# One product for the row shift, and modulation items and weight loads moved around the expert router

## The chip, the cores and the metric

The kernel is one program on one core of a Trainium2 chip. The metric is the device time of one launch in microseconds, the median of three runs. Its engines are TensorE (matrix products and transposes), VectorE, ScalarE, GpSimd and SyncE; SyncE, ScalarE and GpSimd start the transfers between HBM and on-chip memory.

## The reference

One inference step of a backbone with two trunk layers, on 128 context tokens and 512 latent tokens of width 1024:

```
mod = silu(cond) @ mod_w + mod_b          # sh1, sc1, g1, sh2, sc2, g2: 6 x 1024, per group of tokens
h   = rms_norm(x) * (1 + sc1) + sh1       # three mixers: Hyena (two long convolutions), attention, short conv
x   = x + g1 * (merged @ w_o)
h2  = rms_norm(x, norm2_w) * (1 + sc2) + sh2
aff = softmax(h2 @ router_w)              # each of 16 experts takes its best tokens: 16 context, 64 latent
x   = x + g2 * scatter_add(gate * down(silu(a) * u))     # a, u = gathered h2 @ w_gate, w_up
```

The "row shift" is the `+ sh2` of the fourth line, for the rows that are stored to HBM for the experts to gather.

## The kernel before

All weights come from HBM as one stream of items of 128 x 2048 numbers (1 MB), in the order in which TensorE uses them. SyncE asks for them. Four of the places that they land in are `ring`; in the expert stage eight more (`extra`, in the tiles that the trace calls front and back) make it twelve. An item is asked for when the item before it in the same place is used up (`item_used`), and SyncE does so strictly in order.

The kernel runs in stages: a **front** stage, in which the spectra of the long convolutions are made in 20 steps; then for each layer the projections, the attention, the two convolutions (`o` = 0 and 1), the branch and output projections (`w_o`, eight items `c`), the **router** and the 16 **experts** of 6 items each. Between the stages there is no barrier; semaphores set the order, and the code of each engine is written out by hand in the order in which it runs.

The 48 items of `mod_w` (24 per layer) are "modulation items". Each costs TensorE eight 32-column products (`mod_rows`, L777), a copy by ScalarE, and two small products (`mod_columns`, L790 or L792), whose result VectorE or ScalarE adds a bias to. They are needed late, so they are used as filling: `EARLY` of them in the front stage, one or two in each step, and the others (`LATE`, two numbers per layer) in the convolutions and behind the router. The early ones are the 24 of the first layer and those that `LATE` leaves over.

The router stage on TensorE: logits, mean squares, a `spread` of the row scales over all partitions (L758), then ten half tiles of rows. `turn(n)` transposes four 128 x 128 blocks (L1261), `add_shift(n)` adds the shift to them with four full-precision products against diagonal matrices (`diag`, L1267); ScalarE scales the half tile out of PSUM (`evac_t`, L1818), and after each second one stores 128 rows to HBM (`store_rows`, L1824). A `turn` waits until the half tile two before it has been taken out. Meanwhile VectorE finds each expert's best tokens (`best`, `chosen`), which TensorE turns (L1288 to L1294) so that VectorE can write the row numbers `idx`. GpSimd gathers the rows of an expert (L689) when the rows are stored and `idx` is there; `turn_rows` (L1307) turns them, ScalarE and VectorE split them and the weights into a high and a low part, and the expert's products (L1322 to L1352) start.

The router also needs `sh2 @ router_w`: `router_shift` (L1159, sixteen products with 16 columns), which stands between the two halves of the inverse transform of the first convolution (`inverse(0)`, `inverse(1)`, L1174). VectorE takes it into `lbias`.

## Time and profile before

| | |
|---|---|
| median of 3 runs | 2148.35 us (2147.32 to 2151.87) |
| the profiled execution | 2155.39 us, of which 2153.6 us are the span from first to last instruction |
| TensorE busy | 2095.7 us, 97% of the span |
| VectorE, ScalarE, GpSimd busy | 1681.4, 1134.5, 164.2 us |
| moved by the DMA engines | 435.80 MB, 202 GB/s on average |
| granted TensorE clock, mean | 0.989 of full |

A busy TensorE is a TensorE with work in its pipeline; it says nothing of how densely the products follow each other. What a stage is worth is read from its own timeline.

### The profile page before, as it was taken

Reading aid. Unit: us, or ns where it says so; the run is one execution under the profiler, and the core shown is the slowest. Engines: PE = TensorE matmul, PEld = TensorE weight load, DVE = VectorE, ACT = ScalarE, POOL = GpSimd, SP = SyncE. Lnnn points to the kernel's source line nnn. Section 1 sums busy time; section 2 is a strip of 40 time slices with the busy share of each in tenths; the row PEclk is TensorE's granted clock in tenths of the full one; section 3 lists DMA queues with packets and bytes.
Section 4 is the critical chain, followed back from the end, with each engine's and each line's share of the span. In section 5 each row is a group of like instructions: output and inputs, shape, how many; then the busy total and the mean of one; then the engine's idle time right before and its main releaser. Section 6 shows DMA issues by size and latency. Waiting matters only on the chain.

```text
span 2153.6 us, 35885 instructions
## 1 busy us (share of the span) xinstructions
PE 2095.7 (97%) x13286; PEld 1707.6 (79%) x13286; DVE 1681.4 (78%) x2516; ACT 1134.5 (53%) x1798; POOL 164.2 (8%) x192
## 2 busy tenths in 40 slices
PE   8999999999999999999999999999999999999999
PEld 3449999998768997666668999999766999666666
DVE  7767878876768645999997787887777764799997
ACT  5434444324712255888884444433651225788884
POOL 1110000001001100111100000000100100111110
PEclk9999999999999999999999999999999999999999
DMA  9982433213133517999992243222413434999995
GB/s 334 329 305 87 147 136 119 83 75 117 76 118 136 171 62 294 392 382 385 382 354 98 96 147 133 98 82 76 152 42 135 159 130 159 353 378 385 385 386 216
DMA packets 76975, 435.80 MB, mean 202 GB/s; under 512 B 9228, under 2 KB 9900, under 8 KB 36381
## 3 DMA queue, kind: packets, MB, share of 16 engines
q1 hardware_dynamic: 54336, 352.87, 42.7%
q0 software_dynamic: 19024, 72.32, 10.7%
q10 hardware_dynamic: 3470, 8.64, 1.1%
q8 instruction: 96, 1.57, 0.3%
q14 instruction: 49, 0.40, 0.1%
HBM read 384.95 MB, written 48.84 MB: 201 GB/s over the span
## 4 chain that ended last, share of the span: by engine, by line
PE 80%; DVE 8%; ACT 4%; issue 4%; DVEq 2%; DMA 2%; ACTq 0%; POOL 0%; another core or an unknown queue 0%; POOLq 0%
PE ps L738 21%; PE ps L977 17%; PE ps L1322 9%; PE ps L1348 5%; PE ps L1326 4%; PE ps L919 3%; PE ps L1352 2%; PE ps L843 2%; PE ps L1049 2%; DMA kspec<-back 2%; PE ps L777 2%; PE ps L1174 2%; PE ps L1177 1%; PE ps L933 1%; PE ps L1102 1%
## 5 line engine op out<-in xcount | busy, mean ns | idle before, releaser
L738 PE MATMUL ps<-front_r 128*128 128x320 f32 x2432 | 417.0, 310 | 1.6 <-DVE back_r L2474 0.8
L738 PEld LDWEIGHTS ps<-front_r 128*128 128x128 f32 x2432 | 370.1, 188 | 3.0 <-DVE back_r L2474 1.4
L1420 ACT ACTIVATE front_r<-ring 128x1024 fp32r<-128x1024 f32 (+1 forms) x216 | 182.5, 845 | 261.2 <-PE ps L738 172.1
L977 PE MATMUL ps<-back_r,front_r 128*128 128x320 f32 x1728 | 265.1, 309 | 0.0
L977 PEld LDWEIGHTS ps<-back_r,front_r 128*128 128x128 f32 x1728 | 256.4, 188 | 0.0
L1420 ACT ACTIVATE back<-ps 128x512 f32<-128x512 f32 (+5 forms) x206 | 98.5, 496 | 249.6 <-PE ps L738 114.1
L977 PE MATMUL ps<-front_r 128*128 128x320 f32 x1296 | 204.7, 311 | 5.3 <-DVE back L2153 5.1
L977 PEld LDWEIGHTS ps<-front_r 128*128 128x128 f32 x1296 | 191.9, 188 | 10.4 <-DVE back L2153 9.5
L1420 ACT ACTIVATE front_r<-back 128x512 fp32r<-128x512 f32 (+2 forms) x216 | 150.1, 709 | 87.8 <-PE ps L977 35.0
L2588 DVE TENSOR_TENSOR back_r<-front,back_r 128x1024 fp32r<-128x1024 f32 x128 | 153.5, 1220 | 12.4 <-ACT back_r L1420 10.6
L1322 PE MATMUL ps<-back_r 128*80 128x512 f32 x384 | 152.3, 397 | 3.7 <-ACT back_r L1420 3.7
L1322 PE MATMUL ps<-back_r,front_r 128*80 128x512 f32 x384 | 152.3, 397 | 0.0
L738 PE MATMUL ps<-back_r,front_r 128*128 128x320 f32 x640 | 145.8, 309 | 0.0
L2137 DVE TENSOR_TENSOR front_r<-back,front_r 128x512 fp32r<-128x512 f32 x144 | 98.8, 686 | 55.3 <-ACT front_r L1420 55.1
L1420 ACT ACTIVATE back_r<-front 128x1024 fp32r<-128x1024 f32 x128 | 132.9, 1055 | 5.8 <-PE ps L1326 1.0
L1921 DVE TENSOR_TENSOR front_r<-ring,front_r 128x1024 fp32r<-128x1024 f32 x76 | 92.8, 1223 | 42.9 <-ACT front_r L1420 41.8
L1326 PE MATMUL ps<-back_r 128*80 128x512 f32 x384 | 120.5, 395 | 0.0
L2588 DVE TENSOR_TENSOR back_r<-ring,back_r 128x1024 fp32r<-128x1024 f32 x96 | 114.3, 1218 | 2.5 <-ACT back_r L1420 1.2
L738 PEld LDWEIGHTS ps<-back_r,front_r 128*128 128x128 f32 x640 | 107.1, 188 | 0.0
L1348 PE MATMUL ps<-back_r,front_r 128*80 128x512 f32 x384 | 105.7, 397 | 0.0
L1420 ACT ACTIVATE back_r<-ring 128x1024 fp32r<-128x1024 f32 x96 | 99.6, 1055 | 7.1 <-PE ps L1352 4.1
L2153 DVE TENSOR_TENSOR back<-ps,back 128x320 f32<-128x320 f32 x180 | 88.2, 490 | 14.7 <-PE ps L977 2.1
(317 smaller groups left out, 3734.8 us busy)
## 6 DMA issues: line engine op xcount, KB each, us to landing
ring<-in_stream SPq DMA_DIRECT2D x186, 1024.0 KB, 7.9
front<-in_stream SPq DMA_DIRECT2D x80, 1024.0 KB, 16.0
back<-in_stream SPq DMA_DIRECT2D x48, 1024.0 KB, 14.9
gates<-back SPq DMA_DIRECT2D x24, 640.0 KB, 3.1
back<-gates POOLq DMA_DIRECT2D x48, 320.0 KB, 3.3
kspec<-back POOLq DMA_DIRECT2D x20, 512.0 KB, 8.4
front<-kspec POOLq DMA_DIRECT2D x8, 1024.0 KB, 7.7
rows<-front ACTq DMA_DIRECT2D x10, 520.0 KB, 5.4
```

Source lines behind the costliest of these rows:

```text
L738: mm = pe.matmul(tokh(b)[:, c0:c1], w(wp)[:, k, :], src(hp, k)[:, c0:c1], start=first, stop=last)
L777: mm = pe.matmul(ps[32 * j:32 * j + 32, row_bank(i), 0:256], cs[:, k, :], w[:, k, :], start=k < 4, stop=k >= 4)
L919: mm = pe.matmul(qkv_tile(i, t), h_part(hp, 4 * hf + k)[:, P * t:P * t + P], w2(hf, 4, wp)[:, k, :], start=first and hf == 0 and t % 2 == ...
L977: mm = pe.matmul(ps[:, bank, 0:TH], w[:, wp, k, :], x(k), start=k == 0 and wp == 0 and x is hi and j not in (2, 6), stop=k == 3 and wp == ...
L1322: pe.matmul(ps[0:SLOTS, hf, :], x[:, k0 + k, :], hi[:, k, :], start=k0 + k == 0 and x is xe_hi, stop=False)
L1326: mm = pe.matmul(ps[0:SLOTS, hf, :], xe_hi[:, k0 + k, :], lo[:, k, :], start=False, stop=k0 + k == KC - 1)
L1348: pe.matmul(ps[0:SLOTS, 6 + c, :], hidT[i][:, ee % 2, 2 * half + k, :], hi[:, k, :], start=half + k + i == 0, stop=False)
L1420: return act.activation(o, i, ACT.Copy)
L1921: dve.tensor_tensor(half_dst(u, 1), src, half_dst(u, 0).bitcast(F32), ALU.subtract).then_inc(w_lo, 1)
L2137: dve.tensor_tensor(WG[:, n % 4, 1, :], operand(l, n), WG[:, n % 4, 0, :].bitcast(F32), ALU.subtract).then_inc(w_lo, 1)
L2153: dve.tensor_tensor(out[:, dst, :], ps[:, bank, 0:TH], out[:, one, :], ALU.add).then_inc(gate_dve, 1)
L2588: dve.tensor_tensor(w[:, 1, :], part_item(l, ee, v)[1], w[:, 0, :].bitcast(F32), ALU.subtract).then_inc(e_wlo, 1)
```

## The change

It has five parts.

1. The shift of the rows becomes one product. Every number of `sh2` lies in a 16-partition pattern `shift_rows` (made by one product at the end of `router_shift`, with ScalarE copying its operand and VectorE its low part); VectorE spreads it into `spread_rows` at the fourth output item with two products of 96 x 1024. `add_shift` is then one product of the reduced-precision type fp32r with 512 columns, its 96 rows holding high and low parts. The sixteen `diag` activations per layer on ScalarE go. The low part of the spread row scales is a new VectorE operation ahead of the search.
2. `router_shift` moves behind `inverse(1)`, and VectorE's `lbias` copies behind the four products that follow it.
3. SyncE asks for 3 instead of 6 expert items before it waits for the first gather.
4. `LATE` gives the router stage of the first layer 6 instead of 4 modulation items; `EARLY` falls from 29 to 27. The lists of one and two items per step in the front's steps 10 to 19 change from 1 2 2 1 2 2 1 2 2 2 to 1 2 1 2 1 2 1 2 1 2.
5. Three modulation items stand between the last row and the turned places, the others behind them, and then 4 (first layer) or 10 (second) products whose result nobody reads (`keep_busy`).

```diff
-MODS, LATE = DEPTH * N_MOD, ((5, 4), (6, 4))
+MODS, LATE = DEPTH * N_MOD, ((5, 6), (6, 4))
...
+        with nc.sbuf_tensor("shift_rows", [P, QK], F32R) as shift_place:
+            pass
+        shift_rows = shift_place[:, P:2 * P]
...
+        shift_cols = qkw[:, 2 * P:3 * P]
...
-        z, spr, diag = region(56, [KC, T]), region(86, [T]), region(76, [2, KC, P])
+        z, spr, spread_rows = region(56, [KC, T]), region_r(86, [T]), region_r(76, [2, KC, P])
...
                 for x in range(LAP):
-                    if x == 6:
+                    if x == 3:
 
                         sp.wait_ge(gathered[0], l * 64 + 16)
...
-                                mm = pe.matmul(ps[:, 7, 320 + NE * g:320 + NE * g + NE],
+                                pe.matmul(ps[:, 7, 320 + NE * g:320 + NE * g + NE],
                                                mod[:, l, 24 + k, g:g + 1].to_broadcast([P, P]), rw[:, k, :],
                                                start=k == 0, stop=k == KC - 1)
-                        mm.then_inc(r_lg, 1)
+                        pe.wait_ge(sh_hi, 2 * l + 1)
+                        pe.matmul(ps[:, 7, 0:P], shift_cols, ident[:], start=True, stop=True).then_inc(r_lg, 1)
...
                     else:
                         prompt_inverse(0)
+                        pe.wait_ge(rt_lo, 3 * l + 1)
                     forward_second()
...
                     inverse(0, range(4))
                     if o == 0:
                         prompt_forward()
+                    inverse(1, range(4))
+                    if o == 0:
                         router_shift()
-                    inverse(1, range(4))
...
                 def add_shift(n):
                     t, hf = n // 2, n % 2
-                    for i in range(4):
-                        mm = pe.matmul(ps[:, 4 + n % 2, P * i:P * i + P], spr[:, P * t:P * t + P],
-                                       diag[:, int(t > 0), 4 * hf + i, :], start=False, stop=i == 3)
-                    mm.then_inc(t_ready, 1)
+                    pe.matmul(ps[:, 4 + n % 2, :], spr[0:96, P * t:P * t + P],
+                              spread_rows[0:96, int(t > 0), 4 * hf:4 * hf + 4, :].rearrange("p i n -> p (i n)"),
+                              start=False, stop=True).then_inc(t_ready, 1)
...
-                pe.wait_ge(z_ready, l * Z_IN + Z_IN)
+                pe.wait_ge(rt_lo, 3 * l + 3)
                 add_shift(0)
                 add_shift(1)
...
-                pe.wait_ge(r_places, l * 2 + 1)
-                apart(pe)
-                pe.transpose(ps[0:SLOTS, 0, 0:LISTS], places[:], ident[0:LISTS, 0:LISTS])
...
+                def turn_places():
+                    pe.wait_ge(r_places, l * 2 + 1)
...
                 mods = late_mods(l, 1)
-                for i in mods:
+                for x, i in enumerate(mods):
+                    if x == 3:
+                        turn_places()
                     mod_rows(i)
-                    if i > mods[0]:
+                    if x:
                         mod_columns(i - 1)
                 mod_columns(mods[-1])
+                keep_busy(2, 10 if l else 4)
...
                     if o:
+                        act.wait_ge(r_lg, 2 * l + 1)
+                        copy(shift_rows, ps[:, 7, 0:P]).then_inc(sh_hi, 1)
                         act.wait_ge(y_sum, l * 4 + 1)
...
                     late_add(conv_mods(l, o)[-1])
+                    if o == 0:
+                        act.wait_ge(modcol_read, conv_mods(l, o)[-1] + 1)
+                        copy(shift_cols.rearrange("p (j m) -> p j m", j=8), mod[:, l, 24:32, :].rearrange("p k g -> p (k g)")
+                             .unsqueeze(1).to_broadcast([P, 8, 16])).then_inc(sh_hi, 1)
...
-                        act.activation(diag[:, g, k, :], ident[:], ACT.Identity, scale=mod[:, l, 24 + k, g:g + 1])
...
-                    if o == 0:
-                        dve.wait_ge(r_lg, 2 * l + 1)
-                        for g, t0, t1 in ((0, 0, 1), (1, 1, NT)):
...
                     for m in range(4):
                         dve.wait_ge(y_inv, l * 10 + 5 * o + m + 1)
...
                         ins.then_inc(y_out, 1)
+                    if o == 0:
+                        dve.wait_ge(r_lg, 2 * l + 1)
+                        dve.wait_ge(sh_hi, 2 * l + 2)
...
+                        dve.tensor_tensor(shift_rows[64:96, :], ps[64:96, 7, 0:P], shift_rows[64:96, :].bitcast(F32),
+                                          ALU.subtract).then_inc(rt_lo, 1)
...
                 for c in range(KC):
+                    if c == 3:
+                        whole = [96, KC, P]
+                        for g in range(2):
+                            ins = dve.tensor_tensor(spread_rows[0:96, g], shift_rows[0:96, :].bitcast(F32).unsqueeze(1).to_broadcast(whole),
+                                                    sel16[0:96, g:16:2].unsqueeze(2).to_broadcast(whole), ALU.mult)
+                        ins.then_inc(rt_lo, 1)
...
+                dve.wait_ge(z_ready, l * Z_IN + Z_IN)
+                dve.tensor_tensor(spr[32:64, :], spread_at(l, 1)[32:64, :], spr[32:64, :].bitcast(F32),
+                                  ALU.subtract).then_inc(rt_lo, 1)
                 dve.wait_ge(r_affT, l + 1)
```

TensorE around `router_shift` in the first layer (`ps` is PSUM), before:

```order
L1174 MATMUL ps<-front 128x512 x8
L1138 MATMUL ps<-back,csi 128x512 x2
L1159 MATMUL ps<-rw,mod 128x16 x16
L1174 MATMUL ps<-front 128x512 x8
L1102 MATMUL ps<-back,front 128x256 x16
```

and after:

```order
L1180 MATMUL ps<-front 128x512 x8
L1143 MATMUL ps<-back,csi 128x512 x2
L1180 MATMUL ps<-front 128x512 x8
L1164 MATMUL ps<-rw,mod 128x16 x16
L1168 MATMUL ps<-ident,qkw 128x128
L1107 MATMUL ps<-back,front 128x256 x16
```

The sixteen products now follow both inverse halves, with one more behind them.

TensorE from the last half tile of rows to the first gathered rows, first layer, before:

```order
L1261 MATMUL ps<-ident,back 128x128 x4
L1267 MATMUL ps<-back 128x128 x4
L1288 MATMUL ps<-ident,places 80x80
L1289 MATMUL ps<-ident,best 64x80
L1294 MATMUL ps<-back 64x32
L777 MATMUL ps<-ring,cs 32x256 x16
L792 MATMUL ps<-sel,back 128x2 x2
L777 MATMUL ps<-ring,cs 32x256 x8
L792 MATMUL ps<-sel,back 128x2 x2
L777 MATMUL ps<-ring,cs 32x256 x8
L792 MATMUL ps<-sel,back 128x2 x4
L1307 MATMUL ps<-ident,back 128x80 x8
```

and after, from the third modulation item on; three of them now come ahead of the places and three behind, then the four `keep_busy` products, and each group of four shift products has become one (`L1274 MATMUL ps<-back_r 128x512`):

```order
L782 MATMUL ps<-ring,cs 32x256 x8
L797 MATMUL ps<-sel,back 128x2 x2
L1296 MATMUL ps<-ident,places 80x80
L1297 MATMUL ps<-ident,best 64x80
L1302 MATMUL ps<-back 64x32
L782 MATMUL ps<-ring,cs 32x256 x8
L797 MATMUL ps<-sel,back 128x2 x2
L782 MATMUL ps<-ring,cs 32x256 x8
L797 MATMUL ps<-sel,back 128x2 x2
L782 MATMUL ps<-ring,cs 32x256 x8
L797 MATMUL ps<-sel,back 128x2 x4
L771 MATMUL ps<-csi,ident 128x256 x4
```

SyncE's requests from the last items of the trunk on, with what they wait for, before:

```order
L548 DMA ring<-in_stream 128x2048 [waits item_used] x27
L548 DMA front<-in_stream 128x2048 [waits merge_ready]
L548 DMA front<-in_stream 128x2048 x2
L548 DMA back<-in_stream 128x2048 x3
L548 DMA ring<-in_stream 128x2048 [waits r_sub,rows_stored,item_used,t_evac,gathered0]
L548 DMA ring<-in_stream 128x2048 [waits item_used] x3
L548 DMA front<-in_stream 128x2048 x2
```

and after:

```order
L553 DMA ring<-in_stream 128x2048 [waits item_used] x29
L553 DMA front<-in_stream 128x2048 [waits merge_ready]
L553 DMA front<-in_stream 128x2048 x2
L553 DMA back<-in_stream 128x2048 [waits rows_stored,r_sub,t_evac,gathered0]
L553 DMA back<-in_stream 128x2048 x2
L553 DMA ring<-in_stream 128x2048 [waits item_used] x4
L553 DMA front<-in_stream 128x2048 x2
```

The first row has two more modulation items, and the wait for the gather has moved three items ahead.

## Rows read from the trace of the kernel before

**Rows 1.** TensorE timeline in the front stage: start, duration, line, form, idle before

```profile
114.33 1.07 PE L777 MATMUL ps<-ring,cs 128*32 128x256 f32 x16 [0.48 <-ACT back L1420]
...
129.87 0.41 PE L790 MATMUL ps<-ident,back 128*128 128x128 f32 x2 [1.23 <-DVE mod L1975]
...
134.64 0.44 PE L790 MATMUL ps<-ident,back 128*128 128x128 f32 x2
```

**Rows 2.** TensorE timeline, second half of the first convolution and start of the next

```profile
623.71 3.87 PE L1159 MATMUL ps<-rw,mod 128*128 128x16 f32 x32
...
627.42 8.57 PE L1174 MATMUL ps<-front 128*128 128x512 f32 x16
...
635.83 7.07 PE L1102 MATMUL ps<-back,front 128*128 128x256 f32 x32
```

**Rows 3.** stretches: busy us of PE, PEld, DVE, ACT, POOL; PEclk, DMA share, GB/s

```profile
627.00:630.00 3.00, 3.00 (x7) 1.57 (x7) 1.36 (x4) 0.00 (x0) 0.71 (x1) 0.50 0.82 329
...
821.00:824.00 3.00, 3.00 (x18) 3.00 (x18) 1.79 (x9) 1.83 (x4) 0.00 (x0) 0.59 1.00 423
...
842.00:845.00 3.00, 2.90 (x40) 1.81 (x39) 0.00 (x0) 1.21 (x5) 1.46 (x2) 1.00 0.10 15
...
849.00:851.00 2.00, 1.05 (x3) 0.72 (x4) 1.95 (x3) 2.00 (x3) 0.00 (x0) 0.50 1.01 296
```

**Rows 4.** VectorE timeline, end of the second spectrum half

```profile
623.10 1.22 DVE L2414 TENSOR_TENSOR front<-back 128x1024 f32<-128x1024 f32 x1
```

**Rows 5.** VectorE timeline at the fourth output item

```profile
787.92 1.01 DVE L1956 SCALAR_TENSOR_TENSOR X<-ps,mod,X 128x128 f32<-128x128 f32 x2 [3.81 <-PE ps L738]
```

**Rows 6.** TensorE timeline of the router stage, first layer

```profile
828.46 0.60 PE L1261 MATMUL ps<-ident,back 128*128 128x128 f32 x4
...
828.89 1.06 PE L1267 MATMUL ps<-back 128*128 128x128 f32 x8
...
837.77 0.23 PE L1288 MATMUL ps<-ident,places 80*80 80x80 f32 x1
...
842.05 1.07 PE L777 MATMUL ps<-ring,cs 128*32 128x256 f32 x16
...
843.71 1.07 PE L777 MATMUL ps<-ring,cs 128*32 128x256 f32 x16
...
847.31 0.77 PE L1307 MATMUL ps<-ident,back 80*128 80x80 f32 x8 [0.16 <-issue]
...
849.95 0.71 PE L1322 MATMUL ps<-back_r 128*80 128x512 f32 x1 [1.86 <-ACT back_r L1420]
...
852.59 0.63 PE L1322 MATMUL ps<-back_r 128*80 128x512 f32 x1
```

**Rows 7.** ScalarE timeline of the same stage: first pair of rows, last store

```profile
826.33 1.52 ACT L1818 ACTIVATE front<-ps,rstd 128x512 f32<-128x512 f32 x2 [2.12 <-PE ps L1267]
...
838.74 0.33 ACTq L1824 DMA_DIRECT2D rows<-front  x1
```

**Rows 8.** VectorE timeline of the same stage

```profile
825.38 0.42 DVE L2541 COPY back<-ps 80x256 f32<-80x256 f32 x1 [1.18 <-PE ps L1276]
...
837.27 0.17 DVE L2552 CAST places<-chosen 16x16 f32<-16x16 uint32 x1
...
839.41 0.17 DVE L2568 SCALAR_TENSOR_TENSOR idx<-ps,back 64x16 uint32<-64x16 f32 x1
```

**Rows 9.** GpSimd timeline: the first gather of rows

```profile
843.24 0.99 POOL L689 DMA_INDIRECT back<-rows,idx  x1 [94.26 <-DMA rows<-front]
```

**Rows 10.** SyncE timeline: the last two weight items of the first layer

```profile
1097.22 1.70 SPq L583 DMA_DIRECT2D front<-in_stream  x2
```

**Rows 11.** DMA issues of 1098 to 1100: size, time from issue to landing

```profile
front<-in_stream SPq DMA_DIRECT2D x1, 1024.0 KB, 19.8
```

**Rows 12.** TensorE timeline: the first product of the last item

```profile
1129.83 1.13 PE L1348 MATMUL ps<-back_r,front_r 128*80 128x512 f32 x4
```

**Rows 13.** TensorE timeline: the first rows turned for an expert, second layer

```profile
1848.00 0.75 PE L1307 MATMUL ps<-ident,back 80*128 80x80 f32 x8
```

26 lines of the change are left out of this document (15 added, 11 removed).

## The prediction

> **What bounds the kernel now.** I read the profile's page first: TensorE is busy for 97% of the span, so a gain has to come out of its timeline or out of something that it waits for. Then the timelines of TensorE stage by stage, beside them those of the engines that release it, and last the transfers.
>
> In the front stage TensorE is the bound, with stalls on top. A modulation item costs it 1.28 us there (114.33 to 115.33 for the eight products, and the two small ones take it to the next product 0.27 us later), and in the later steps it waits 0.48 us for ScalarE and 1.23 us for VectorE [rows 1]. In the convolution it runs without a gap: `router_shift` takes 3.7 us, `inverse(1)` 8.4 us, and the next transform follows at once [rows 2]. The granted clock was 0.50 from 627 to 630, that is 1.2 instead of 2.4 GHz, right behind the sixteen narrow products [rows 3]. The operand of `inverse(1)` was ready only at 624.32 [rows 4]. At the output items VectorE idles 3.8 us in 7 [rows 5].
>
> In the router stage I look for what comes last ahead of the first expert product. A half tile costs TensorE 0.43 us for `turn` and 0.90 us for `add_shift` [rows 6], 13.3 us for ten; ScalarE takes 0.76 us per half tile and about 0.4 us for a store, so it waits for TensorE; the last store is asked for at 838.74 [rows 7]. VectorE starts the search at 825.38, has the places at 837.4 and `idx` at 839.6 [rows 8]; GpSimd starts to gather only at 843.24, released by the last store [rows 9]. So the rows come last, by 3.6 us. The gathered rows are turned at 847.31, the first expert product starts at 849.95, and the clock is 0.50 there [rows 3, 6]. In the expert stage TensorE never waits for weights. But the last item, asked for at about 1098.7 [rows 10], lands 19.8 us later [rows 11], at 1118.5, for a product at 1129.83 [rows 12]; its ScalarE and VectorE passes take some 1.8 us ahead of it (the low part is needed later), so the stream has only 9.5 us to spare. In the second layer the same stage starts at 1848.00 [rows 13], and I take its slack as the first's.
>
> **The change part by part.**
>
> *Two items fewer in the front.* 2 x 1.28 = 2.6 us of TensorE. The two stalls, 1.7 us together, lie in steps behind the removed items, and 2 MB less are in flight by then; I take 1.4 of them. Sum -4.0; ends -2.6 (TensorE alone) and -7 (the same relief once more elsewhere).
>
> *`router_shift` behind `inverse(1)`.* TensorE's work is the same plus one full-precision product of 128 columns, 0.23 us by the four in 0.90 us [rows 6]. But `inverse(1)` would start at 623.87 and its operand is there at about 624.45: 0.6 us of idle time that `router_shift` covered. The slow spell cost about 1.7 us of the work behind it (3.4 us at half speed); it can land on the next transform in the same way, or not come. I take +0.3 per layer, +0.6 in all; ends -0.5 and +1.2 per layer. The new waits: ScalarE stands at `r_lg` with only its copy of the spectrum behind it, which waits for TensorE's transform, 3.5 us later, anyway. VectorE's copies and its low part (about 0.5 us) fall in the same pause. Cost nothing.
>
> *The spreading on VectorE*, twice 96 x 1024: 2.4 us, since an operation on 128 x 1024 takes 1.22 us [rows 4], and it fits under 3.8 us of idle time [rows 5]. The `diag` activations that go were hidden too. Both nothing; without the cover +2.4 per layer.
>
> *One product per half tile.* A product of 512 columns in fp32r is paced at 0.23 us [rows 12]: TensorE needs 0.43 + 0.23 = 0.66 us, and ScalarE becomes the bound with 2.0 us per pair including the store. It starts 0.6 us earlier and takes 10 us: last store at 835.4 instead of 838.74. GpSimd saw the stored rows 4.5 us after the last request, so now at 839.9 instead of 843.24. The new VectorE operation (640 columns, 0.8 us at the pace of [rows 4]) fits into the 1.2 us that VectorE waits ahead of 825.38.
>
> *Three modulation items ahead of the places.* They pace at 1.66 us each, 842.05 to 843.71. TensorE is free at 834.2, ScalarE's first copy waits for its last store, so the third ends at 839.5; the places were ready at 837.4. The places are turned 1.7 us later than at 837.77, `idx` comes at 841.3, and the gather starts at about 841.6. Now `idx` comes last, 1.6 us earlier than the rows did. The places' own late turn is what is next in line.
>
> *What follows them.* First layer: three more items, 840.5 to 846.6, then four products of 256 columns at 0.44 us (16 take 7.1 in L1102's rows, 0.44 each [rows 2]): TensorE reaches `turn_rows` at 848.3, the gathered rows are there by 845.7 if the gather takes 4.1 us as before (843.24 to 847.31), by 847.5 beside five loads. +1.0 against 847.31. Second layer: one item and ten such products, 847.6: -0.5 against 1848.00.
>
> *The clock.* Before, TensorE idles much between 845 and 850, and the first two weight parts then take 2.64 us each (849.95 to 852.59 is the first) [rows 6]. Six products at 0.23 would take 1.4, and VectorE's pass over a part 1.2: 2.5 us lost per layer. The added products fill the idle time up to the turned rows, but 1.9 us without any product remain behind them. I take -1.7 per layer, nearer to the whole since one slow spell may stay; ends 0 and -2.5. The Trainium skill (TensorE: Matmul & The Clock Gate, Loop structure matters more than you think) says that a copy out of PSUM by VectorE between groups of products does not make the array go cold, while a wait for a DMA does. By that the whole 2.5 would come back, -1.6 us more in all; no row before shows it or excludes it, and it is part of the rival "more".
>
> *The held items.* An item is 1.05 MB at 423 GB/s, 2.5 us [rows 3]. Second layer: three items not there beforehand are 7.5 us, the gather comes 1.2 us earlier, so the stream ends 6.3 us later, TensorE's need is 2.2 us earlier: 8.5 of 9.5 us. No wait. First layer: five (two of modulation), 12.5 us, of which the DMA engines' pause before (15 GB/s from 842 to 845 [rows 3]) gives back some 5: 7.5 to 9, against 9.5 - 0.7. I take +0.3 and +0.5 for the partial sums, which are loaded behind the last item. The Trainium skill (DMA: Bandwidth & Descriptors, Where 436 GB/s comes from) puts the HBM side of one core at about 358 GB/s. By that an item would take 2.9 us and the five of the first layer 2.1 us more, which comes out as waiting; it speaks for the rival "eaten up". The trace has 423 GB/s, and the measurement decides.
>
> Sum: -4.0 + 0.6 + (1.0 - 1.7 + 0.8) + (-0.5 - 1.7) = -5.5 us. The profiled execution would be 2155.4 - 5.5 = 2149.9; it lies 7 us over the median of the runs shown, so for the median I take the difference: 2148.35 - 5.5 = **2142.9**.
>
> **The rivals.** 0.2% (4.3 us) is about what a measurement of this kernel tells from no change.
>
> *Eaten up.* The stream is the bound of the first layer: the gather shares the engines with five loads, lands at 849.5, and the end waits 3 us; the clock falls as before in both layers. For it: 9.5 us of slack against 7.5 to 9. Against it: TensorE is not free before 848.3 anyway. -4.0 + 0.6 + (2.2 + 3.0) + (-0.5) = +1.3 with no clock back, -4.0 + 0.6 + (1.0 - 1.0 + 3.0) + (-0.5 - 1.0) = -1.9 with some: about 2147 (2145 to 2150).
>
> *The rows stage goes cold (slower).* TensorE ran through the rows without a pause; now it waits a third of a microsecond for ScalarE in each half tile. The clock fell behind narrow products and pauses three times in these rows (0.50 at 627, 0.59 at 821, 0.50 at 849) [rows 3]; whether short regular pauses do it too, no row shows. If they do, `turn` and product take 1.3 us, the rows end 3.5 us later than I say, and each of the three items ahead of the places takes 2.0 us instead of 1.0 in its products, 3 us more. Then the places are turned at 846 instead of 837.8, and the gather starts 5 us later than at 843.24, in both layers: -4.0 + 0.6 + 2 x 5 = +6.6, 2155. Against it: the clock was full from 827 on, through transposes and modulation items with pauses of their own. It decides only if both layers' stages are slow throughout; one alone ends at +1.6.
>
> *More.* Both spells of the convolutions vanish (-0.5 each instead of +0.3), the clock comes back whole, the front gives 6: -6 - 1.0 + (1.0 - 2.5 + 0.8) + (-0.5 - 2.5) = -10.7: 2137.7.
>
> **How the numbers follow.** Forecast (2139 to 2146) 0.50; eaten up 0.28; cold rows 0.12; more 0.10. The range from 2137 to 2150 leaves out the cold rows and a little of the last. Faster by over 0.2% (under 2144.05): 0.45 of the forecast and 0.10, 0.55. Within: 0.05 and 0.28, 0.33. Slower: 0.12.
>
> **What the profile of the changed kernel would show.** Right: the spread product 0.23 us per half tile, half tiles 1.0 us apart with ScalarE as releaser, the last store near 835.4 on this scale, the places turned about 839.5, the first gather released by VectorE and not by a store, an expert stage that starts at a granted clock of 1.00 or falls to 0.50 more briefly; the front 4 us shorter; latencies of the last weight items near 27 us and still no wait for a landing. Wrong: a clock of 0.50 between 825 and 845; expert products that wait for weight passes held up by a transfer; a gather still released by a store.

## The result

The changed kernel is slower: 2161.97 us (median of 4, 2160.24 to 2163.45) against 2147.84 us (median of 4 on the same chip). The ratio is 1.0058 with a 95% interval of 1.0046 to 1.0071. By the ratio that is 12.5 us, and the two medians lie 14.1 us apart, where -5.5 was forecast. Its profiled execution took 2160.24 us, with a span of 2158.4. The execution of before whose rows stand above was one of its longest (2155.39 us), so the two traces differ by less, 4.8 us, and only that much (8.6 us against the second profile) can be followed stage by stage. A second profile of the kernel before (2151.59 us, span 2149.8) stands beside it in this table; the times are starts of TensorE's instructions, in us.

| | before, rows above | before, second profile | after |
|---|---|---|---|
| first layer: places turned | 837.8 | 837.0 | 835.2 |
| gathered rows turned | 847.3 | 847.5 | 847.4 |
| first expert product | 849.95 | 850.16 | 850.55 |
| last expert product | 1133.8 | 1133.8 | 1137.8 |
| second layer: places turned | 1837.9 | 1835.8 | 1842.9 |
| gathered rows turned | 1848.0 | 1844.5 | 1852.6 |
| last expert product | 2134.2 | 2130.4 | 2139.0 |

So the lead of 3.0 us (2.3 against the second profile) with which the changed kernel comes to the first router stage is gone between the places and the first expert product. From the turned places to the turned rows it takes 12.2 us, where before took 9.5 and 10.5. The expert stage then takes 287.3 us instead of 283.8 and 283.6. In the second layer the way from the places to the rows is 9.7 us, where before took 10.1 and 8.6.

**What the changed kernel's profile shows.** SyncE's timeline (start, duration of the group, line, tile, number of transfers) in the first layer:

```profile
803.29 30.24 SPq L553 DMA_DIRECT2D ring<-in_stream  x3
833.58 1.57 SPq L553 DMA_DIRECT2D front<-in_stream  x3
846.70 1.28 SPq L553 DMA_DIRECT2D back<-in_stream  x3
```

The three `ring` transfers were asked for over 30 us: the first at 803.29, the other two, modulation items five and six, not before 831.4 and 833.2. The expert items behind them on the queue follow at 833.58. What the transfers did meanwhile is in the stretches (length, TensorE busy, granted clock, DMA share, GB/s), first of the changed kernel:

```profile
808.00:831.00 23.00, 21.34 (x165) 0.93 0.21 84
831.00:850.00 19.00, 14.40 (x132) 0.81 1.00 353
```

The same stretches in the second profile of before:

```profile
808.00:831.00 23.00, 22.48 (x180) 0.93 0.70 281
831.00:850.00 19.00, 13.78 (x148) 0.96 0.71 242
```

From 808 to 831 the changed kernel moved 84 GB/s (the stores of the rows, nearly all of it) where before moved 281. From 831 on its engines are full, just when the gather comes. GpSimd's timeline at the first gather:

```profile
837.90 1.02 POOL L694 DMA_INDIRECT back<-rows,idx  x1 [91.91 <-DVE idx L2596]
```

The DMA issues (transfers, KB each, us to landing) of 833.4 to 835:

```profile
front<-in_stream SPq DMA_DIRECT2D x3, 1024.0 KB, 15.1
```

And those of 837.5 to 838.5:

```profile
back<-rows,idx POOLq DMA_INDIRECT x1, 8.8
```

The gather is asked for at 837.90, released by VectorE's `idx` and no longer by a store [rows 9]. It takes 8.8 us to land, and an expert item takes 15.1 us (the middle one of three). TensorE's timeline shows what the stage makes of that:

```profile
830.25 1.07 PE L782 MATMUL ps<-ring,cs 128*32 128x256 f32 x16
...
835.21 0.24 PE L1296 MATMUL ps<-ident,places 80*80 80x80 f32 x1
...
838.47 1.07 PE L782 MATMUL ps<-ring,cs 128*32 128x256 f32 x16 [0.69 <-DMA ring<-in_stream]
...
840.81 1.07 PE L782 MATMUL ps<-ring,cs 128*32 128x256 f32 x16 [0.73 <-DMA ring<-in_stream]
...
843.86 3.76 PE L771 MATMUL ps<-csi,ident 128*128 128x256 f32 x8
847.41 1.27 PE L1318 MATMUL ps<-ident,back 80*128 80x80 f32 x8
850.55 0.71 PE L1333 MATMUL ps<-back_r 128*80 128x512 f32 x1 [1.86 <-ACT back_r L1431]
...
852.34 1.05 PE L1337 MATMUL ps<-back_r 128*80 128x512 f32 x2
```

The two late modulation items wait for their own transfers (0.69 and 0.73 us). The filling products, four of 256 columns in eight records, take 3.76 us, twice the 1.76 of the prediction, because they ran at half clock. The gather had landed at 846.68, 0.7 us before the rows were turned at 847.41: it was TensorE's own chain that came last. The granted clock in these stretches, and in those of the second layer:

```profile
840.00:843.00 3.00, 1.69 (x21) 0.97 1.02 406
843.00:850.00 7.00, 5.67 (x20) 0.50 1.03 308
1843.00:1846.00 3.00, 2.05 (x25) 1.00 0.00 0
1846.00:1850.00 4.00, 3.90 (x12) 0.57 0.57 137
```

The first layer's spell at 0.50 began at 842.8 and lasted 13.7 us, where before had 6.8 from 848.8. TensorE had not stood for more than 0.8 us at a time in the ten microseconds ahead of its fall. In the second layer's timeline the ten filling products (20 records) end behind the landing of the first gathered rows, which was at 1849.70:

```profile
1846.75 6.03 PE L771 MATMUL ps<-csi,ident 128*128 128x256 f32 x20
1852.62 0.72 PE L1318 MATMUL ps<-ident,back 80*128 80x80 f32 x8
```

In the expert stage ScalarE now waits for weights. Its waits from 850 to 1135 (released by, us in total, times, longest):

```profile
ACT back_r L1431 <- DMA ring<-in_stream: 4.1, 3, 1.6
...
ACT back_r L1431 <- DMA back<-in_stream: 1.4, 3, 0.8
```

No such wait is in either profile of before. TensorE's timeline where the longest of them reaches it:

```profile
1045.80 1.14 PE L1359 MATMUL ps<-front_r 128*80 128x512 f32 x4 [1.19 <-DVE front_r L2633]
```

The stages that came nearest to what was foreseen are the front and the convolution. TensorE's timeline in the front:

```profile
109.53 0.41 PE L795 MATMUL ps<-ident,back 128*128 128x128 f32 x2 [0.52 <-DVE mod L1991]
...
127.24 0.41 PE L795 MATMUL ps<-ident,back 128*128 128x128 f32 x2 [1.70 <-DVE mod L1991]
...
131.01 0.50 PE L825 MATMUL ps<-b,rows 40*128 40x512 f32 x2
```

And in the first layer's convolution:

```profile
620.39 7.13 PE L1180 MATMUL ps<-front 128*128 128x512 f32 x16 [0.50 <-DVE front L2430]
627.36 3.64 PE L1164 MATMUL ps<-rw,mod 128*128 128x16 f32 x32
...
631.16 8.76 PE L1107 MATMUL ps<-back,front 128*128 128x256 f32 x32
```

There are still two such stalls as in [rows 1], 0.52 and 1.70 us, and TensorE's waits up to 140 us are no shorter in sum (12.6 us; 12.4 and 11.9 before). The product that stands at 131.01 stood at 135.01 in the rows above, but at 132.60 in the second profile of before. `inverse(1)` waits 0.50 us and the narrow products still bring the clock down, now over the next transform, which takes 8.76 us instead of 7.07 [rows 2].

### The profile page after: what moved, and what is told of

It is laid out like the page before. It is cut to its first block, busy times and chain, and to the rows that moved or that the text cites. A ratio compares the mean times of both kernels' runs of the same rounds, so it can differ in the third digit from the quotient of the medians.

```text
span 2158.4 us, 35657 instructions
## 1 busy us (share of the span) xinstructions
PE 2095.1 (97%) x13182; PEld 1702.1 (79%) x13182; DVE 1686.5 (78%) x2520; ACT 1126.0 (52%) x1774; POOL 165.8 (8%) x192
## 4 chain that ended last, share of the span: by engine, by line
PE 71%; DMA 9%; DVE 8%; ACT 5%; issue 4%; DVEq 3%; ACTq 0%; POOL 0%; SPq 0%; POOLq 0%
PE ps L743 21%; PE ps L982 17%; PE ps L1333 6%; PE ps L1359 4%; DMA ring<-in_stream 3%; PE ps L1337 3%; PE ps L924 3%; DMA back<-in_stream 2%; DMA kspec<-back 2%; PE ps L1363 2%; PE ps L1054 2%; PE ps L1183 1%; DMA front<-in_stream 1%; PE ps L848 1%; PE ps L1107 1%
## 5 line engine op out<-in xcount | busy, mean ns | idle before, releaser
L2616 DVE TENSOR_TENSOR back_r<-front,back_r 128x1024 fp32r<-128x1024 f32 x128 | 153.5, 1221 | 12.5 <-ACT back_r L1431 10.7
```

The source lines that it names most:

```text
L2616: dve.tensor_tensor(w[:, 1, :], part_item(l, ee, v)[1], w[:, 0, :].bitcast(F32), ALU.subtract).then_inc(e_wlo, 1)
```

## The experiments

All ratios are to the kernel before, timed in turn with it on the same chip. Runs that are compared with each other were not always on one chip, so they are compared by their ratios. 0.1% is 2.15 us. The "held items" are the expert items that SyncE asks for ahead of its wait for the first gather. In the later groups "bare" means without the filling products and with `router_shift` between the transforms again.

**e1_before**: the kernel before once more.

> The kernel before, unchanged, for a second profile on this chip. Its first profiled execution took 2155.39 us and the median of the others was 2148. If the difference of 7 us is a stage of its own (a slower stream, one more spell at half clock), it shows when the two traces are laid side by side: the stage in which they part is where executions of this kernel differ. Expected: 2148, parted from the first profile in the expert stages or in the number of spells at half clock.

Its profiled execution took 2151.59 us. The two traces of one kernel lie 2.4 us apart at the end of the front stage, level again in the first expert stage, 1.6 us apart at the second convolution, 2.0 at the second layer's rows and 3.6 at its gathered rows. The spells at half clock are not the same either: one at 612.9 is new, one at 1613.4 is gone. So an execution's place in 2147.5 to 2155 is made of many small waits and spells, no single stage. One profile against one profile can't tell less than some 5 us here, and the verdicts below go by the ratios.

### The queue: six modulation items and four slots

```diff
 # e4_ahead: the changed kernel, three held items ahead of modulation items five and six
+                    if l == 0 and g >= first - 2:
+                        continue
                     load(g)
...
                     if x == 3:
+                        if l == 0:
+                            load(first - 2)
+                            load(first - 1)
                         sp.wait_ge(gathered[0], l * 64 + 16)
 # e5_four_more: the kernel before with LATE = ((5, 6), (6, 4))
 # e13_four_more_behind: the same with the edit of e4_ahead, at x == 6
 # e2_four: the changed kernel with LATE = ((5, 4), (6, 4))
 # e3_six_held: the changed kernel with x == 6
```

> The changed kernel with one thing moved on SyncE's queue: in the first layer the three held expert items are asked for ahead of modulation items five and six instead of behind them. Bytes, items and TensorE's order are the same. 'Held back': the three land by 832 as before, 7.5 us of stream are won in the pause from 808 to 831, the gather has two items ahead of it instead of five and lands in 4 to 6 us instead of 8.8 to 12.9; TensorE starts the expert stage 1 to 3 us earlier and does not wait for the stream (-3.4): -4.5 to -6.5, about 2156.5. 'Volume': no difference, 2162. 'Clock': no difference, the products that fill are there as before, within 1 us of 2162.

Measured: 1.0019 (1.0010 to 1.0029), 2154.7 us. The order of five transfers on one queue is worth 0.39%, 8 us, with no byte and no product changed. SyncE's timeline:

```profile
801.21 0.33 SPq L553 DMA_DIRECT2D ring<-in_stream  x1
810.98 1.28 SPq L553 DMA_DIRECT2D front<-in_stream  x3
829.38 2.16 SPq L553 DMA_DIRECT2D ring<-in_stream  x2
840.11 1.28 SPq L553 DMA_DIRECT2D back<-in_stream  x3
```

The three expert items are asked for at 811 and not at 833.6. The gather, asked for at 835.91, landed at 840.09, in 4.2 us instead of 8.8, and in the whole expert stage ScalarE waits for no landing. TensorE itself did not turn the rows before 846.09, since modulation item six (1.63 us late) and the fill lay ahead of them. Its timeline:

```profile
839.09 1.07 PE L786 MATMUL ps<-ring,cs 128*32 128x256 f32 x16 [1.63 <-DMA ring<-in_stream]
...
842.54 3.76 PE L775 MATMUL ps<-csi,ident 128*128 128x256 f32 x8
846.09 1.14 PE L1322 MATMUL ps<-ident,back 80*128 80x80 f32 x8
849.09 0.46 PE L1337 MATMUL ps<-back_r 128*80 128x512 f32 x1 [1.86 <-ACT back_r L1435]
```

The places were turned at 833.21, so the way to the rows is 12.9 us, no shorter than the changed kernel's 12.2, though the gather took half the time. What the order gave back in this trace is the expert stage: 283.0 us instead of 287.3.

> The kernel before with nothing changed but the place of two modulation items: six in the first layer's router stage instead of four, 27 in the front. 'Held back': -4.0 in the front, but the six expert items wait behind items five and six, whose slots come free only behind the places, at about 840; they land from 845 on, the gather lies behind eight transfers, TensorE gets the first weights and the rows some 10 us late and the stream bounds the stage: +5 or more in all, 2153 or more. 'Volume': 5 us of stream out of 9.5 us of slack, no wait: -4, 2144.

Measured: 1.0045 (1.0032 to 1.0059). Two items moved on the kernel before cost 10 us, with the front's gain already taken off. SyncE stood from 802.2 to 835.8, the gather took 11.4 us, the first expert product came at 853.0, and the expert stage took 289.4 us, with 8.1 us of ScalarE's waits for landings.

> e5_four_more (1.0045) with all six held expert items asked for ahead of modulation items five and six. Two items more in the first layer's router stage, on the kernel before, with nothing else in their way but the ring's slots. 'Held back': the expert items land by 832 as before, the two late modulation items are asked for at 836 to 838 and the gather shares the engines with them: turned 2 to 4 us later than before, front -4: ratio 0.999 to 1.000. If it stays at 1.0045, the order on SyncE's queue is not what e5_four_more lost, but the two items' own work and bytes.

Measured: 1.0016 (1.0006 to 1.0026). The same two items with the queue in order: 6 us better, ScalarE waits for no weights, but not the gain that I expected. In its trace, that of the longest of its eleven executions, the gather still takes 7.7 us beside the two late items and the rows are turned 15.4 us behind the places (9.5 before): TensorE waits 2.49 us for item six and turns the rows 2.1 us after they have landed. Both readings hold in part: 0.29% is the order, the rest the two items themselves, their transfers and TensorE's wait for them.

> The changed kernel with four modulation items in the first layer's router stage again (29 in the front), all else as changed. Theory 'held back': SyncE issues the stream in order, the ring has four slots, and items five and six wait for a slot that TensorE frees only behind the rows, so the expert items behind them are late (their first landing was at 849.3 where before it was at 820.9). Four items fit the ring: the first expert items are asked for at about 816 again, the gather lands in 4 us, no product waits for the stream. Against the changed kernel +4.0 in the front, -3.4 in the expert stage, -3 ahead of the first expert product: about -2.5, 2159.5. Rival 'volume' (two items more, three not held: the bytes are what is late): the same two items leave the expert stage, -3.4, and nothing ahead of it: +0.6. Rival 'clock' (the products that fill the wait run at half speed and cost more than the wait): +4.0 alone, 2166.

Measured: 1.0026 (1.0015 to 1.0038), 7 us under the changed kernel. I expected 2.5 and the sign is right. The first layer's gather landed in 3.97 us. The expert stage still took 286.4 us, and ScalarE waited 4.6 us for landings. The first layers of e6_no_fill and e7_conv, also with three held, took 286.1 and 286.3 us; with four held and the same four modulation items it was 282.9 to 284.7 (b2, e11, e12, e15). e4_ahead took 283.0 with three, but its first expert product came 9.0 us after the gather had landed, where e2_four's came after 2.8. So three held items are too few for the stream once TensorE comes early.

> The changed kernel with six expert items ahead of SyncE's wait again instead of three. 'Held back': the three more cannot be asked for before modulation item six has its slot, at 833 to 835, so they lie ahead of the gather (asked for at 837.9) with 7.5 us of transfers: the gather lands near 854 instead of 846.7, the first expert product comes 3 to 6 us later, and the stream, which then never pauses for the gather, gives back the 3.4 us of waits: 0 to +3 against the changed kernel, 2162 to 2165. 'Volume' (three items fewer in advance are what the stream lacks): -3.4, about 2158.5.

Measured: 1.0045 (1.0029 to 1.0062), against 1.0058. That is nearer to what 'volume' said (1.0042) than to 'held back' (1.0058 or more), and the interval reaches both. Items four to six were not asked for before 836, as foreseen, but the gather did not wait for them: it took 8.5 us, hardly less than beside the five, and the way from places to rows stayed at 12.3 us. My theory had the gather 7 us later, and that was wrong. The stream still bounded the expert stage (286.4 us, 3.7 us of ScalarE's waits).

### The filling products, the convolution

```diff
 # e6_no_fill: e2_four without
-                keep_busy(2, 10 if l else 4)
 # e7_conv: e2_four with router_shift() ahead of inverse(1) again
```

> Four modulation items in the first layer, and the products that fill the wait for the gathered rows left out (they compute nothing that is used). Compared with e2_four (1.0026 of before). 'The fill is in the way': in the second layer of e2_four the gathered rows landed at 1846.98 and TensorE turned them only at 1852.90, behind ten such products in 7.6 us at half clock; in the first layer the rows landed at 844.36 and were turned at 844.40. So -4 to -6 from the second layer, nothing from the first: ratio to before about 1.0002. Rival 'the fill keeps the clock': without it the expert stages start at half clock for 2.5 us longer in both layers: +3 and -5 give -1 to -2, ratio about 1.0018.

Measured: 1.0017 (1.0008 to 1.0026), 2 us under e2_four, with intervals that overlap. That is the rival's number (1.0018). In the trace the second layer's way from places to rows fell from 12.6 to 6.8 us; the same trace has 13.7 us at 0.50 from 1838.6, and its expert stage is 1.0 us longer. So one trace shows the fill in the way and some of it paid back by the clock, but by the times its going is worth 0.09%, which the error covers.

> Four modulation items in the first layer, and the products of the router's shift between the two inverse transforms again instead of behind the second; compared with e2_four (1.0026). There TensorE waited 0.50 us ahead of the second inverse transform in the first layer and the narrow products brought the half-clock spell all the same, now over the next transform: 1.0 us lost in the first layer and some 1 to 1.5 in the second. Back in the old order: -2, ratio about 1.0017. Rival (the price lies in the added product and the new waits of ScalarE and VectorE, whatever the place): 0, ratio 1.0026.

Measured: 1.0019 (1.0011 to 1.0028), again 1.5 us under e2_four and inside its interval. From the second half's first transform to its last the first layer took 21.7 us in four of five runs with the new order (20.1 in the fifth) and 21.0 in most with the old one, but 22.4 to 22.7 in three; the second layer 21.0 to 23.8 and, but for one, 20.7 to 22.6. By the means the move costs 0.15 us in the first layer and 1.2 in the second, too little to be shown by a time.

### The one product alone: what a pause costs

```diff
 # e9_product: bare, four modulation items, six held, and turn_places() ahead of all of them
+                turn_places()
                 for x, i in enumerate(mods):
-                    if x == 3:
-                        turn_places()
 # e10_third_six: the same with turn_places() behind the third item
 # e11_first_four: e9_product with x == 4
 # e14_filled_pause: e9_product with
+                keep_busy(2, 9)
                 turn_places()
```

> The one product per half tile alone on the kernel before: four modulation items in the first layer, all of them behind the places, six expert items held, the router's shift between the inverse transforms, nothing that fills. TensorE has the rows done some 5 us earlier. Theory 'the stores queue behind the held items': with six items asked for ahead of them the last store took 10.46 us to land in b1_six_ahead (asked for at 830.52, landed 840.99), against 2.65 us for most stores with three held; so the gather starts hardly earlier than before, 1 us at most per layer: -1 to -2, ratio 0.9992. Rival 'the rows came last' (as the prediction had it): gather 1.6 to 3 us earlier per layer, the modulation items behind the places end at the same time as the rows land: -4 to -5, ratio 0.998.

Measured: 1.0040 (1.0028 to 1.0052). Both theories fell: less work for TensorE made the kernel 8.6 us slower. TensorE's timeline in the second layer:

```profile
1829.90 0.47 PE L1274 MATMUL ps<-back_r 96*128 96x512 f32 x1
1834.57 0.33 PE L1296 MATMUL ps<-ident,places 80*80 80x80 f32 x1 [4.19 <-DVE places L2578]
...
1835.81 1.93 PE L782 MATMUL ps<-ring,cs 128*32 128x256 f32 x16
1838.34 1.94 PE L782 MATMUL ps<-ring,cs 128*32 128x256 f32 x16 [0.59 <-ACT back L1429]
...
1848.29 1.31 PE L1316 MATMUL ps<-ident,back 80*128 80x80 f32 x8
```

The rows are done at 1830.3, the places come from VectorE at 1834.6. TensorE stood for 4.19 us, and from 1833.7 the granted clock was 0.50 for 20.5 us: a modulation item's products take 1.94 us where they took 1.07, four items take until 1848, and the rows that landed near 1842.6 wait for them.

> e9_product with one thing changed: three modulation items ahead of the places instead of none (six expert items held, four modulation items in the first layer, nothing that fills, the router's shift between the transforms). Theory 'TensorE idles behind the rows': in e9_product it stood 4.3 us before the places, the clock was 0.50 from 833.6 to 840.4 and from 847.3 to 854.1 in the first layer and for 20.5 us from 1833.7 in the second, and the modulation items and the first weights ran at half speed; with the items in that pause the spells are shorter and most of the 8 us come back: ratio 1.000 to 1.0015. Rival 'the price is in the product and its helpers' (copies, spreading, new waits): 1.0040 as e9_product.

Measured: 0.9998 (0.9988 to 1.0007). Three modulation items in the pause, nothing else changed, are worth 0.42%.

> b2_four_held (0.9987) with one thing changed: the places ahead of all four modulation items, so e9_product with four held expert items instead of six. 'TensorE idles behind the rows': the pause of 4.3 us is there again, the clock falls: ratio 1.002 to 1.004. Rival 'the stores behind the held items' (what e9_product lost lies in the six held): 0.998 to 0.999, as b2_four_held or better, since the places are turned 1 us earlier.

Measured: 1.0039 (1.0024 to 1.0053). With b2_four_held (0.9987, below) this makes a square: places first 1.0040 and 1.0039, places third 0.9998 and 0.9987, at six and four held. The pause is the price; the stores behind six held items instead of four cost some 0.1%, with intervals that overlap.

> e9_product (1.0040) with nine products that nobody uses in TensorE's pause between the last row and the places: 9 x 0.44 = 4.0 us at the full clock, in a pause of 4.3 us. No work that counts is moved: the four modulation items stay behind the places. If the clock is what the pause costs, most of it comes back: ratio 1.000 to 1.001, as e10_third_six (0.9998), and the spells at half clock behind the pause get shorter. If e10_third_six gained because three modulation items lie out of the way of what follows the places (5 us of work earlier), this one stays at 1.0035 to 1.0045.

Measured: 1.0006 (0.9998 to 1.0015). Four microseconds of products that nobody uses make e9_product 7 us faster. No other work moved, so it is the clock. By the traces nearly all of it is in the second layer, where the way from the places to the first expert product falls from 16.9 to 12.4 us; in the first layer it is 12.8 and 13.0, since the rows there were ready only 1.0 us before e9_product turned them. The same timeline:

```profile
1828.47 4.05 PE L771 MATMUL ps<-csi,ident 128*128 128x256 f32 x18
1832.68 0.24 PE L1296 MATMUL ps<-ident,places 80*80 80x80 f32 x1 [0.16 <-DVE places L2579]
...
1833.65 1.07 PE L782 MATMUL ps<-ring,cs 128*32 128x256 f32 x16
1835.31 1.07 PE L782 MATMUL ps<-ring,cs 128*32 128x256 f32 x16 [0.59 <-ACT back L1430]
...
1841.91 1.33 PE L1317 MATMUL ps<-ident,back 80*128 80x80 f32 x8 [0.40 <-DMA back<-rows,idx]
```

The stretch from 1833 to 1854 (columns as above) in e9_product:

```profile
1833.00:1854.00 21.00, 15.93 (x98) 0.52 0.75 272
```

and in e14_filled_pause:

```profile
1833.00:1854.00 21.00, 17.01 (x123) 0.84 0.78 283
```

The granted clock is 0.52 against 0.84. The items take 1.07 us again and TensorE is at the rows when they land.

### Toward a version that keeps the gains

```diff
 # b1_six_ahead: bare, six modulation items, six held items ahead of the last two of them
 # b3_ahead_bare, b4_ahead_four: the same with three and with four held
 # b2_four_held: bare, four modulation items, four held (x == 4)
 # e12_second_four: b2_four_held with turn_places() behind the second item
 # e15_short_fill: b2_four_held with keep_busy(2, 4) behind the last item
```

> What the theory would keep: the one product per half tile and six modulation items in the first layer, but all six held expert items asked for ahead of modulation items five and six, no products that fill, and the router's shift between the inverse transforms. Against e4_ahead (1.0019): -3 from the second layer's fill, -2 to -3.5 from the first's (rows landed at 840.1, turned at 846.1), -2 from the convolutions, and three items more in hand for the stream: ratio 0.9975 to 0.9985, about 2146. If the stream is what bounds it even so, ratio 1.000.

Measured: 1.0014 (1.0005 to 1.0023), no gain: with six transfers ahead of them the stores took 7.4 to 10.5 us, the gather was asked for 4 us later than in the changed kernel (841.89), and half clock lasted 17.1 us.

> e4_ahead (1.0019: six modulation items, three held expert items asked for ahead of items five and six) without the products that fill and with the router's shift between the inverse transforms. In e4_ahead the gathered rows landed at 840.09 and were turned at 846.09 in the first layer, at 1843.45 and 1846.52 in the second. Expected -3 and -3 for these and -1.5 for the convolutions, and 2 us of them taken back by the stream, which then bounds the first layer's expert stage: ratio 0.9990. If a colder clock or the stream takes all of it back, 1.001 to 1.002.

Measured: 1.0008 (0.9999 to 1.0018), between the two.

> The same with four held instead of three. If the stream bounds the first layer's expert stage in b3_ahead_bare, -2 against it, ratio 0.998 to 0.999; if not, the same as b3_ahead_bare. Against it stands that the first store waits for the fourth item to land, 1 to 2 us, which costs something only if the last store still comes after the places.

Measured: 0.9995 (0.9985 to 1.0005). The fourth held item shows no difference from b3_ahead_bare that the intervals could carry.

> Four modulation items in the first layer, four expert items ahead of SyncE's wait instead of three, nothing that fills, the router's shift between the inverse transforms. e6_no_fill and e7_conv were 1.0017 and 1.0019 with one of the two edits each; both together give about 1.0010. The stage from the first expert product to the last took 286.1 and 286.3 us there against 283.6 to 283.8 in the kernel before: the stream bounded it by 2.5 us. The fourth item is asked for at 816 and lands near 827.6, just as the first store is asked for, so it should give back up to 2.5 us and cost the stores nothing: ratio 1.0000. If the number held is not what the stream lacks, 1.0010.

Measured: 0.9987 (0.9977 to 0.9997), 2147.91 us: the one version that is faster than the kernel before, by 2.8 us, less than the 0.2% that I set as the bound. It is the best of seventeen versions, and its interval ends at 0.9997, so a part of this may be chance. The expert stage is back at 282.9 us. TensorE's timeline shows what is left:

```profile
836.54 0.24 PE L1296 MATMUL ps<-ident,places 80*80 80x80 f32 x1
...
843.69 1.33 PE L1317 MATMUL ps<-ident,back 80*128 80x80 f32 x8 [3.39 <-DMA back<-rows,idx]
846.87 0.71 PE L1332 MATMUL ps<-back_r 128*80 128x512 f32 x1 [1.86 <-ACT back_r L1430]
...
848.66 1.05 PE L1336 MATMUL ps<-back_r 128*80 128x512 f32 x2
```

TensorE waits 3.39 us for the gathered rows and starts the experts at half clock, as the kernel before did [rows 6].

> b2_four_held with two modulation items ahead of the places instead of three. The places are ready some 0.8 us before TensorE turns them in b2_four_held. With two they are turned 0.8 us earlier in each layer and the gather starts so much earlier, since the stores have landed by then; TensorE waits less than 1 us ahead of them: ratio 0.998, 1 to 1.5 us under b2_four_held. If the short pause lets the clock fall, 0.9995.

Measured: 0.9993 (0.9983 to 1.0003), not told apart from b2_four_held. A pause of about half a microsecond ahead of the places (0.49 us in the second layer) did not bring the clock down.

> b2_four_held (0.9987) with four filling products ahead of the gathered rows in both layers. There TensorE waited 3.39 us for the rows in the first layer and 1.44 us in the second; four products are 1.76 us at the full clock and 3.7 us at half. If a fill that fits into the wait keeps the clock for the first weights: 0.9975 to 0.9985. If the clock has fallen already and the fill only delays: +2 in the second layer, 0.9995 or a little more.

Measured: 0.9991 (0.9980 to 1.0001). In its trace, that of the longest of its twelve executions, the second layer's experts start at the full clock, but the time doesn't tell it from b2_four_held. ScalarE waits 3.1 us for landings in the first layer, none in b2_four_held; that TensorE, started sooner, runs into the stream there is my reading and not shown. A fill that fits the wait kept the clock here, and what it gives is not seen in the time.

## Why the prediction was wrong

**The step that failed first** is that of the held items: "First layer: five (two of modulation), 12.5 us, of which the DMA engines' pause before gives back some 5". It counted bytes. I had quoted no row of SyncE's queue ahead of 847, and took it that items five and six, and the held three, are asked for when they were before. The ring has four slots. Item five waits on the queue for TensorE's first modulation item of this stage, at 831.4, and everything behind it waits with it. In the pause that was to give something back, the stream stood for 23 us. What I entered as +0.8 came to +3.5 in the expert stage (287.3 us against 283.8), and with the same items asked for in another order e4_ahead took 283.0. The second place where it shows is the way from the places to the rows, for which I had 8.8 us (839.5 to 848.3) and which took 12.2: 1.4 us of the difference are TensorE's waits for the transfers of items five and six, and 2.0 us are the filling products at half clock, which belong to the next step. Against the stage's beginning the rows came 3.1 us later than before (2.2 by the second profile), where +1.0 was predicted. The slow gather (8.8 us) was over 0.7 us before; without the other two it would have been the next bound. The rival "eaten up" had this sign and place, 3.0 us of waits, and still placed the end at 2147.

**The clock** is the second step that failed: "-1.7 per layer". I took the filling products to keep it up. They came when it had fallen, took twice their time in the first layer (3.76 us) and 6.03 instead of 4.4 in the second, and ended 2.9 us behind the landing of the rows there. What was to be won was the first weight parts, 5.2 us for two at half clock: in the changed kernel's first layer they took 5.2 again, and turning the rows and the first wait 0.5 us more than before; in the second they took 4.6. So the term was +0.5 and -0.6 instead of twice -1.7, with the fill's 2.0 and 1.6 us over its sum on top. e6_no_fill puts the price of the fill at 0.09%, within its error. I looked for pauses only between short products in the rows stage (the rival "the rows stage goes cold"). The clock stayed at 1.00 through those, with waits of 0.2 us. In the changed kernel it fell later, at 842.8 and 1846.3, behind modulation items with waits of 0.5 to 0.7 us between them. In e9_product, with no items ahead of the places, it fell right behind the rows, where the shorter stage leaves TensorE idle for 4.2 us; the modulation items ahead of the places fill just this pause. That the shorter rows need those items there I did not see.

**The convolution**: +0.3 per layer, measured from 20.8 us before: +1.0 in the first in four of five runs (-0.7 in the fifth) and +0.2 to +3.0 in the second. The added idle time was as said (0.50 us); the spell did land on the next transform, and on top of it a second one came in e2_four and e6_no_fill (6.8 us at 0.50).

**The front**: the step from 135.01 to 131.01 looks like the 4.0 us of the prediction, but that is luck. The last front step starts at 132.3 us on average in the twelve traces with 29 early items (129.6 to 135.0, and 135.01 is the latest) and at 130.2 in the eight with 27: 2.1 us. The two items' own 2.6 us cover that; the 1.4 us from the stalls do not show.

**Right by its steps**: the router stage begins 3.0 us earlier than before, and on the scale of before the last store was asked for at 834.1 (835.4 predicted), the places were turned at 838.2 (839.5), and the gather was asked for at 840.9 (841.6), released by `idx`. The product takes 0.33 us and not 0.23, the `turn` ahead of it 0.35 and not 0.43: 0.68 us per half tile against 0.66. The spreading on VectorE and the other moved copies cost nothing that shows. All of it is a gain of 2.3 us ahead of the gather, lost to what stood on the queues and on TensorE behind it.

The first rule of the Trainium skill that I weighed (TensorE: Matmul & The Clock Gate, Loop structure matters more than you think) sets VectorE's copies, which do not make the array cold, against a wait for a DMA, which does; in its example the next products do not wait for the copy. The traces here do not part by the engine that is waited for: a wait of 4.19 us for VectorE brought the clock to 0.50 in e9_product. By the second (DMA: Bandwidth & Descriptors, Where 436 GB/s comes from) the stream would have had to slow to about 358 GB/s. It moved 391 GB/s from 850 to 950 and 383 from 950 to 1050, before and after; what it lacked was time.

What stays open: the parts' ratios do not add (1.0045 for the two items alone, 1.0040 for the product alone, 1.0058 for the whole); that each fills or opens a pause of the other is my reading and was not tested. How much of the changed kernel's 12.5 us is clock and how much stream is shown only for the order of the queue (0.39%), and of these 8 us the traces show 4.3 in the expert stage. The remainder is 0.19%; without the fill and with `router_shift` in its old place it is 0.08%, an interval that reaches below 1 (b3_ahead_bare). No run takes the fill alone out of a kernel with six modulation items.

## What to carry to other kernels

Before moving transfers past a point, list what stands on the issuing queue and which slot each entry waits for; one more item than the ring has slots turns a prefetch into a wait for everything behind it. Before shortening a stage of TensorE, look at what comes next: if it is a wait for another engine of some microseconds, the time saved becomes idle time and then half clock for the work behind it, unless useful work is moved into the pause at the same time. Fill waits with work that is needed; products for nothing helped here in one case, where they started before the clock had fallen and ended with the wait (e14_filled_pause), and in the changed kernel, started too late, they ran at half clock and ended behind what was waited for.

## What the runs showed of the hardware

- Nine idle products in a pause of 4.2 us made a kernel 7 us faster (1.0040 to 1.0006). Without them the clock stayed at 0.50 for 20.5 us in the second layer, through four modulation items, the wait for the turned rows and the first products of the experts.
- A row store of 520 KB took 2.65 us on free queues and 7.7 to 9.1 us behind six items of 1 MB that another queue had asked for 8.5 us and more before the first of them (e9_product).
- The first gather of rows took 3.9 to 4.5 us on its own in all traces but one (4.9), 7.7 beside two such items in e13_four_more_behind but 4.2 in e4_ahead, where these had been asked for 3 us sooner, 8.8 beside five, 8.5 beside seven in e3_six_held, and 11.4 in e5_four_more, where eight had been asked for from 2.6 us before it to 2.6 us after it.
- The granted clock fell to 0.50 at 842.8 in the changed kernel, though no idle time of TensorE in the ten microseconds ahead was longer than 0.8 us.
